# Side work spread over the attention steps, value products behind the transposes, three norm sums as rounded pairs

## What is computed

```python
x = _layernorm(x, ln_in_g, ln_in_b)
h = x * (1.0 + scale[:, 0, None, :]) + shift[:, 0, None, :]
y = _swiglu(h, ffn1_w_in[l], ffn1_w_out[l])                       # D_FF = 2816
x = _layernorm(ALPHA * x + 0.5 * gate[:, 0, None, :] * y, post_ln_g[l, 0], post_ln_b[l, 0])

h = x * (1.0 + scale[:, 1, None, :]) + shift[:, 1, None, :]
cq, ckv, k_rope_raw, u = jnp.split(h @ w_in[l], split_at, axis=-1)
attn = _mla(cq, ckv, k_rope_raw, positions, q_norm_g[l], kv_norm_g[l], w_uq[l], w_ukv[l])
pooled = _multiscale_pool(u, pool_w[l], pool_b[l], pool_scale[l])
y = jnp.concatenate([attn, pooled], axis=-1) @ w_out[l]
x = _layernorm(ALPHA * x + gate[:, 1, None, :] * y, post_ln_g[l, 1], post_ln_b[l, 1])
...
```

## Time and profile before

| | |
|---|---|
| median of three runs | 970.99 us (970.50 to 972.26) |
| the profiled execution: its time | 971.01 us |
| the profiled execution: span from first to last instruction | 969.1 us |
| TensorE busy in the span | 951.6 us (98%) |
| VectorE / ScalarE / GpSimd busy | 500.1 / 375.3 / 248.6 us |
| mean granted TensorE clock | 0.997 |

### The profile page before, as it was taken

One profiled execution on the slowest core, in us unless ns is written; L12 is line 12 of the kernel. 1 busy time (PEld: TensorE's weight loads), 2 busy tenths in 40 slices (PEclk: granted clock), 3 DMA queues, 4 the chain that ended last, 5 costly groups with the idle time before them and its releaser, 6 DMA issues.

```text
span 969.1 us, 10730 instructions
## 1 busy us (share of the span) xinstructions
PE 951.6 (98%) x4182; PEld 758.5 (78%) x4182; DVE 500.1 (52%) x701; ACT 375.3 (39%) x549; POOL 248.6 (26%) x213
## 2 busy tenths in 40 slices
PE   7999999999999999999999999999999999999997
PEld 4788888888888888787766686888888888888884
DVE  5956767454565854667656477722232323233333
ACT  6752232333222323675585447532323222222122
POOL 0021111111106321236944463611111111135123
PEclk9999999999999999999999999999999999999999
DMA  9836565656553653212511112332323232223302
GB/s 361 350 121 205 190 202 189 200 174 218 176 179 125 232 185 125 76 66 87 152 45 44 44 66 78 98 108 90 106 90 106 87 109 82 81 77 103 120 17 87
DMA packets 37474, 127.20 MB, mean 131 GB/s; under 512 B 4016, under 2 KB 4144, under 8 KB 37424
## 3 DMA queue, kind: packets, MB, share of 16 engines
q1 hardware_dynamic: 37424, 126.52, 39.2%
HBM read 123.36 MB, written 2.10 MB: 129 GB/s over the span
## 4 chain that ended last, share of the span: by engine, by line
PE 90%; DVE 3%; ACT 3%; issue 2%; POOL 2%; DMA 1%; SPq 0%; POOLq 0%; ACTq 0%; DVEq 0%
PE bank L572 28%; PE bank L574 27%; PE bank L573 27%; PE bank L707 1%; PE bank L915 1%; PE bank L891 1%; PE bank L657 1%; PE bank L651 1%; PE bank L658 1%; POOL cq L1884 1%; DMA x<-xT 1%; POOL q_sum L1841 0%; DVE nmax L1709 0%; POOL x L1892 0%; DVE w_lo L995 0%
## 5 line engine op out<-in xcount | busy, mean ns | idle before, releaser
L995 DVE TENSOR_TENSOR w_lo<-raw,w_hi 128x1024 fp32r<-128x1024 f32 x159 | 216.9, 1370 | 289.8 <-ACT w_hi L987 289.3
L572 PE MATMUL bank<-h_hi,w_hi 128*128 128x512 f32 x727 | 285.3, 392 | 0.0
L574 PE MATMUL bank<-h_hi,w_lo 128*128 128x512 f32 x727 | 283.0, 389 | 0.0
L573 PE MATMUL bank<-h_lo,w_hi 128*128 128x512 f32 x727 | 282.9, 389 | 0.0
L987 ACT ACTIVATE w_hi<-raw 128x1024 fp32r<-128x1024 f32 x159 | 162.4, 1032 | 197.7 <-PE bank L574 196.8
L1791 POOL TENSOR_TENSOR a_lo<-act_t,a_hi 128x512 fp32r<-128x512 f32 x44 | 59.0, 1340 | 423.4 <-ACT a_hi L1081 423.4
L572 PEld LDWEIGHTS bank<-h_hi,w_hi 128*128 128x128 f32 x727 | 136.7, 188 | 28.5 <-issue 0.7
L574 PEld LDWEIGHTS bank<-h_hi,w_lo 128*128 128x128 f32 x727 | 136.5, 188 | 28.7
L573 PEld LDWEIGHTS bank<-h_lo,w_hi 128*128 128x128 f32 x727 | 136.6, 188 | 28.2 <-issue 0.5
L572 PE MATMUL bank<-a_hi,w_hi 128*128 128x512 f32 x352 | 138.6, 394 | 0.0
L574 PE MATMUL bank<-a_hi,w_lo 128*128 128x512 f32 x352 | 137.0, 389 | 0.0
(11 more groups left out here) (293 smaller groups left out, 1023.7 us busy)
## 6 DMA issues: line engine op xcount, KB each, us to landing
raw<-wunits SPq DMA_DIRECT2D x145, 512.0 KB, 3.2
ada_ring<-ada_w SPq DMA_DIRECT2D x56, 512.0 KB, 4.5
ada_first<-ada_w SPq DMA_DIRECT2D x16, 512.0 KB, 10.4
raw<-wunits SPq DMA_DIRECT2D x16, 384.0 KB, 2.9
x<-xT SPq DMA_DIRECT2D x4, 512.0 KB, 5.6
outT<-x SPq DMA_DIRECT2D x8, 256.0 KB, 2.5
K<-k_rope SPq DMA_DIRECT2D x2, 512.0 KB, 8.6
c_act<-c_rows SPq DMA_DIRECT2D x1, 512.0 KB, 7.6
```

The lines of the kernel that those rows point to most:

```text
L572: mm(out, lh, rh, start=first, stop=False)
L573: mm(out, lh, rl, start=False, stop=False)
L574: return mm(out, ll, rh, start=False, stop=last)
L995: nc.vector.tensor_tensor(lo, raw[:, slot, 0:width], hi.bitcast(F32), SUB).then_inc(s_lo, 1)
```

## The change

Five edits, of which the first four lie in the attention loop.

- Fills: of the 20 halves two move. The second half of q6 goes from step 19 to 20, the first half of p3 from step 27 to 26; the steps 11, 19 and 27, which hold a `values`, have no fill after that.
- Values: on PE `values` moves from between the scores and the transposes of its step to behind the transposes (and the fill).
- Weight splits in the loop: each 128x1024 unit is split in two halves of 512 columns, `w_hi` in steps with s % 6 = 0 and 1 (new `act_hi_half`), `w_lo` in steps with s % 6 = 2 and 3 (new `dve_lo_half`). Six units are concerned.
- Residual: the affine of the eight tiles on ACT goes from steps 4 to 11 to steps 1, 2, 3, 5, 8, 9, 10, 11. On POOL four subtractions of the shift go from steps 20, 21, 22, 23 to 22, 23, 24, 25, and one from 27 to 28.
- Norm sums: `s_sum` of norm 1, and `s_sum` and `q_sum` of norm 3 are split like the weights: ACT copies the sum to float32r into a tile of `h_hi` that is free then, POOL writes the rest into the tile of `h_lo` behind it, and PE multiplies both parts (float32r) where it had one float32 product. `q_sum` of norm 1 and both sums of norm 2 stay.

```diff
-FILL_STEP = [3 * i // 2 for i in range(2 * len(FILL))]
+FILL_STEP = [0, 1, 3, 4, 6, 7, 9, 10, 12, 13, 15, 16, 18, 20, 21, 22, 24, 25, 26, 28]
...
+        SPLIT_SUMS = {1: [(s_sum, KD - 1)], 3: [(s_sum, 0), (q_sum, 1)]}
...
             def stats_begin(p):
+                split = SPLIT_SUMS.get(p, [])
                 pe.wait_ge(s_acc[p], 2 * (KD - 2))
-                mm(bank[MEAN[p]][:], ones_d[:], s_sum[:], start=True, stop=False)
-                mm(bank[SQR[p]][:], ones_d[:], q_sum[:], start=True, stop=False)
+                if split:
+                    pe.wait_ge(s_sl[p], len(split))
+                for i, (out, total) in enumerate(((bank[MEAN[p]], s_sum), (bank[SQR[p]], q_sum))):
+                    if i < len(split):
+                        m = split[i][1]
+                        mm(out[:], ones_d[:].bitcast(F32R), h_hi[:, m, :], start=True, stop=False)
+                        mm(out[:], ones_d[:].bitcast(F32R), h_lo[:, m, :], start=False, stop=False)
+                    else:
+                        mm(out[:], ones_d[:], total[:], start=True, stop=False)
...
-                if step >= 11 and step % (2 * QB) == 3:
-                    values((step - 11) // (2 * QB))
...
+                if step >= 11 and step % (2 * QB) == 3:
+                    values((step - 11) // (2 * QB))
...
+            def sums_high(p):                           # ACT, in the last tile of the down projection
+                for i, (total, m) in enumerate(SPLIT_SUMS[p]):
+                    act.wait_ge(s_acc[p], 2 * (KD - 2) - 1 + i)
+                    fn(h_hi[:, m, :], total[:], ACT.Copy).then_inc(s_sh[p], 1)
...
-                if step % 6 == 0 and step < 36:
-                    act_hi(act, S_FILL + step // 6 + LEAD)
+                if step % 6 in (0, 1) and step < 36:
+                    act_hi_half(act, S_FILL + step // 6 + LEAD, step % 6)
...
-                if step % 6 == 2:
-                    lo_after(S_FILL + step // 6)
+                if step % 6 in (2, 3):
+                    dve_lo_half(dve, S_FILL + step // 6 + LEAD, step % 6 - 2)
...
+                for i, (total, m) in enumerate(SPLIT_SUMS.get(p, [])):
+                    pool.wait_ge(s_sh[p], i + 1)
+                    tt(h_lo[:, m, :], total[:], h_hi[:, m, :].bitcast(F32), SUB).then_inc(s_sl[p], 1)
```

More of the change, by code:

```diff
@@ L72 @@
 FILL = ["q2", "q3", "q4", "q5", "p0", "p1", "q6", "q7", "p2", "p3"]
-FILL_STEP = [3 * i // 2 for i in range(2 * len(FILL))]
+FILL_STEP = [0, 1, 3, 4, 6, 7, 9, 10, 12, 13, 15, 16, 18, 20, 21, 22, 24, 25, 26, 28]
 SHIFT_STEP = FILL_STEP[2 * FILL.index("p0") + 1] + 3
-SHIFTED_AFTER = {18: 0, 19: 1, 20: 4, 21: 5, 22: 6, 23: 7, 27: 2, 30: 3}
-AFFINE_STEP = 4
+SHIFTED_AFTER = {18: 0, 19: 1, 22: 4, 23: 5, 24: 6, 25: 7, 28: 2, 30: 3}
+AFFINE_STEPS = [1, 2, 3, 5, 8, 9, 10, 11]
 LAST_POOL = (1, 2, 3)
@@ L423, in build @@
         s_mh, s_ml = sem("attn_hi"), sem("attn_lo")
+        s_sh = {p: sem(f"sums_hi{p}") for p in (1, 3)}
+        s_sl = {p: sem(f"sums_lo{p}") for p in (1, 3)}
+        SPLIT_SUMS = {1: [(s_sum, KD - 1)], 3: [(s_sum, 0), (q_sum, 1)]}
         block = ctx.enter_context(nc.Block())
@@ L988, in act_hi, with act_hi_half, dve_lo_half @@
                 .then_inc(s_hi, 1)
+        def act_hi_half(act, n, part):
+            slot, cols = n % RAWS, slice(UNIT // 2 * part, UNIT // 2 * (part + 1))
+            if part == 0:
+                act.wait_ge(s_raw[slot], 16 * (n // RAWS + 1))
+                act.wait_ge(s_used, w_before(n))
+            half = nc.scalar.activation(parts(n, 0, UNIT)[0][:, cols], raw[:, slot, cols], ACT.Copy)
+            if part == 1:
+                half.then_inc(s_hi, 1)
+        def dve_lo_half(dve, n, part):
+            slot, cols = n % RAWS, slice(UNIT // 2 * part, UNIT // 2 * (part + 1))
+            if part == 0:
+                dve.wait_ge(s_hi, n + 1)
+            hi, lo = parts(n, 0, UNIT)
+            half = nc.vector.tensor_tensor(lo[:, cols], raw[:, slot, cols], hi[:, cols].bitcast(F32), SUB)
+            if part == 1:
+                half.then_inc(s_lo, 1)
         def dve_lo(dve, n):
@@ L1109, in ffn @@
                             act_hi(act, n)
+                        if m == KD - 1 and j == 0:
+                            sums_high(p)
                 preload(2 + f, ACT.Abs_reciprocal_sqrt if f else ACT.Ln)
@@ L1254, in _ @@
                         .then_inc(s_te, 1)
-                if step % 6 == 0 and step < 36:
-                    act_hi(act, S_FILL + step // 6 + LEAD)
+                if step % 6 in (0, 1) and step < 36:
+                    act_hi_half(act, S_FILL + step // 6 + LEAD, step % 6)
                 if step in (4, 6):
                     pool_high(step // 2)
-                if AFFINE_STEP <= step < AFFINE_STEP + KD:
-                    m = step - AFFINE_STEP
+                if step in AFFINE_STEPS:
+                    m = AFFINE_STEPS.index(step)
                     fn(x[:, m, :], x[:, m, :], ACT.Identity, scale=cols[:, C_LNG + KD + m:C_LNG + KD + m + 1],
```

## The result

| | before | changed kernel |
|---|---|---|
| median of six runs | 970.99 us (970.50 to 972.26) | 965.40 us (965.08 to 965.71) |
| the profiled execution, span | 969.1 us | 963.5 us |
| TensorE busy in the span | 951.6 us | 949.3 us |

The ratio of the changed kernel to the one before is 0.9942, 95% interval 0.9931 to 0.9953: faster by 5.6 us, 0.6%. The forecast was 965.7 us, range 964.2 to 967.8.

What follows compares the result with a forecast made beforehand. TensorE was taken to bound the kernel, so only less work or fewer stalls there pay. Loop gains of 4.1 us, 5.3 with the norm sums, take 971.0 to 965.7 us, range 964.2 to 967.8.

Steps and rivals of the forecast that it cites:

- What bounds the kernel, and that gains pass through: Whole kernel: TensorE bounds it, busy 951.6 of 969.1 us; time won earlier is not given back in the long product stages.
- Norm sums: Down projections: three float32 products of 0.86 become float32r pairs of 0.45, none waited for; 1.2 us, range 0.9 to 1.2.
- Step 9: Attention loop, stall of 1.50 before the scores: half a `w_hi` and moved affines let the exp start earlier; gain 1.3 us.
- Step 15: Attention loop, stall of 0.60 before the scores: half of a `w_hi` leaves the chain to the exp; gain 0.4 us.
- Step 19: Attention loop, wait of 0.42 before the values: the transpose fills 0.1 of it, 0.3 is left standing.
- Step 27: Attention loop, stall of 0.90 before the values: covered by half a fill now in step 26; gain 0.9 us.
- Steps 23 and 24: Attention loop, stalls of 1.00 before scores (VectorE) and 0.3 before transposes (GpSimd): both go, gain 1.3 us.
- The end of the loop: Stall of 0.83 before the transposes of step 34, behind the last normalisation on GpSimd: gain 0 to 0.45, taken as 0.1.
- The list of stalls: Attention loop, TensorE: seven stalls read from starts against paces, before steps 9, 15, 19, 23, 24, 27 and 34, 5.55 us.
- Extra starts: Attention loop: each halved split costs a second start, about 0.1 us on ScalarE, less on VectorE, twelve times, off TensorE's path.
- Rival 1: Attention loop: with TensorE earlier, just-in-time work becomes late and half the loop's gain is lost; 967.8 us, chance 15%.
- The sum of the loop: Attention loop: gains of 1.3, 0.4, 1.0, 1.3 and 0.1 add to 4.1 us of the 5.55 of stalls.

Runs made afterwards that it cites:

- old_values: The changed kernel with the value products back between the scores and the transposes, fills keeping their new steps: 965.35 us.
- values_alone: The kernel before with one edit, the value products behind the transposes and the fill of their step: 969.99 us.
- fills_alone: The kernel before with one edit, the halves of q6 and p3 moved (steps 19 to 20 and 27 to 26): 968.69 us.
- old_fills: The changed kernel with the old table of fills (second half of q6 in step 19, first half of p3 in step 27): 966.33 us.
- old_shifts: The changed kernel with the eight subtractions of the shift on GpSimd back in their old steps: 965.50 us.
- late_shift: The changed kernel with the last subtraction on GpSimd behind the last normalisation (step 31 in place of 30): 964.58 us.
- sums_only: The kernel before with the three norm sums as rounded pairs, the attention loop as before: 969.88 us.

## Why the prediction was right, step by step

- **What bounds the kernel, and that gains pass through**: right. The product stages are as full as before.
- **Norm sums**, 1.2 us: 1.1 alone, 1.3 when taken from the changed kernel (966.71 - 965.40). 0.40 per pair, no wait.
- **Step 9**, 1.3 taken of 1.50: all of it went. Against the start of the loop the exp came 1.54 us earlier, at the upper end of 1.16 plus up to 0.4. The cause was right: the affines hold 1.21, the half `w_hi` 0.42, and they overlap.
- **Step 15**, 0.4 of 0.60: all went. The halves give 0.46, and the place of the values the rest: 0.17 comes back in `old_values`, and 0.15 goes in `values_alone`. A term short by 0.2, since the prediction saw no gain from the values there.
- **Step 19**, 0.1 of 0.42: right, 0.32 is left.
- **Step 27**, 0.90: right, and by the half fill in step 26, as the step said. Leaving the values where they were would have cost that step nothing.
- **Steps 23 and 24**, 1.3 for 1.34: the size was right and the list of causes was not, so this term came out in part by luck. The prediction took three things off the chain, the emptying of q6, half a `w_lo` and the blocking by the moved subtractions. The runs show that the moved fill alone does all of both steps (`fills_alone`), the meeting with GpSimd included. What failed is "half the `w_lo` goes behind the next maximum, and the four subtractions leave". The subtraction that met `w_lo` stands behind the normalisation of step 19 and was never moved; the meeting went because, with q6 no longer in front, `w_lo` started first. The half that goes behind the next maximum stands ahead of the one after it, 0.49 in `old_fills` and 0.21 in `old_shifts`. The moved subtractions only keep that half free of a meeting. And the stall of step 24, which the prediction put down to GpSimd alone, had ScalarE's copy 0.1 us behind as a second cause.
- **The end of the loop**, 0.1: nothing, 0.79 of 0.83 stays. The last normalisation still took its turn behind the subtraction and beside a half `w_lo`, 1.65 us in place of 0.70 (1.67 in the kernel before); `late_shift` removes it all.
- **The list of stalls** left out two, 0.37 in step 6 and 0.25 in step 33; the change did nothing for either, so the sum did not suffer.
- **Extra starts**: the prediction put 0.1 us on ScalarE and less on VectorE for a halved split. Two halves took 2 x 0.52 for 0.95 on ScalarE and 2 x 0.68 for 1.22 on VectorE, 0.1 more on either.
- **Rival 1**, that stalls move on, did not come in the changed kernel. `old_fills` shows it on a small scale, as the 0.49 before the scores of step 24; the rest of its 1.19 us are the old stalls of steps 23 and 24, which had never gone.
- The sum of the loop, 4.1, is short by 0.2 of the measured 4.3; with that the forecast was 0.3 us too high.

## What to carry to other kernels

Where one engine bounds a kernel and its stalls are of a microsecond, read them one by one as starts against paces, follow each to the instruction in front of the late one, and move that instruction; what it costs elsewhere is the room of the engine it lands on. When two edits cover the same wait, price them together: here either the fills or the values would have freed step 27. Ask of each moved instruction which later ones start earlier, since they may win or lose a race with another engine. And when several edits are meant to remove one stall, run each by itself and without each: here one moved half fill did what was put down to three edits.

## What was not expected of the hardware

VectorE's split and GpSimd's instructions block one another for nearly a whole instruction, and the one that starts first is not slowed: 2.37 against 1.21 us for a `w_lo` that starts together with a subtraction, 1.58 against 0.70 for a normalisation that starts 0.18 us after a `w_lo`, which itself takes its usual 1.21. The Trainium skill (SBUF — State Buffer, Who interferes with whom) says: "Issue order, not op shape, decides who blocks." The traces agree where one starts clearly first. They add that at equal recorded starts (524.38 and 524.38 in `values_alone`, 522.02 and 522.02 in `old_fills`, 524.58 and 524.58 in `sums_only`) it was VectorE that waited, in all three.

A float32 product of 512 columns over 128 rows took 0.86 us and a pair of float32r products of the same size 0.46, with no cost that shows for a change between the types. At norm 1 the float32 product starts 0.23 after the second of the pair (387.11 to 387.34), and the second float32r product behind it 1.09 later (387.34 to 388.43), which is 0.86 + 0.23.
